# Identity products on TensorE in the two waits at the end of the last head's triangular inverse

## What is computed

```python
def gated_delta_rule(q, k, v, g, beta):
    ...
    lower = jnp.where(tri_strict, jnp.einsum('bhncd,bhnsd->bhncs', k_beta, k) * decay, 0.0)
    ...
    sol = lax.linalg.triangular_solve(lower, rhs, left_side=True, lower=True, unit_diagonal=True)
    ...

        c = depthwise_conv(c, conv_dw_w[i]) + conv_dw_b[i]
        c = jax.nn.silu(layer_norm_2(c, conv_ln_g[i], conv_ln_b[i]))
        y_conv = c @ w_conv_out[i]
        ...
        o = rms_norm_2(o_fwd + o_bwd, delta_norm_g[i]) * jax.nn.silu(z.reshape(bsz, t_len, N_HEADS, HEAD_DIM_2))
        y_delta = o.reshape(bsz, t_len, DELTA_W).astype(x.dtype) @ w_delta_out[i]
```

## Time and profile before

| | |
|---|---|
| time, median of 3 runs | 1242.95 us (1240.95 to 1244.08) |
| span of the profiled execution, first to last instruction | 1239.0 us |
| PE busy | 1211.3 us, 98% |
| DVE busy | 846.4 us, 68% |
| ACT busy | 703.4 us, 57% |
| POOL busy | 300.7 us, 24% |
| PE's share of the chain of work that ended last | 85% |

### The profile page before, as it was taken

How to read it: one execution, slowest core, us unless ns; L and a number is a source line. 1 busy time by engine, 2 the same in 40 slices (tenths; PEclk the granted TensorE clock), 3 DMA queues, 4 the chain that set the end, 5 groups by cost and what they waited for, 6 DMA issues and landing times.

```text
span 1239.0 us, 21308 instructions
## 1 busy us (share of the span) xinstructions
PE 1211.3 (98%) x8590; PEld 1109.0 (90%) x8590; DVE 846.4 (68%) x1507; ACT 703.4 (57%) x1181; POOL 300.7 (24%) x251
## 2 busy tenths in 40 slices
PE   9999999999999999999999999999999999999997
PEld 7776899998877799998899999999988989999886
DVE  6796588874675678885558787788853555555457
ACT  5465576663467566664466666767665445444344
POOL 2170100000024000000166667565645210000000
PEclk9999999999999999999989999999998999999999
DMA  7633355555553355555333232232223555555542
GB/s 282 239 140 138 119 210 194 204 186 175 180 190 108 141 210 206 196 183 203 137 136 136 103 137 103 103 137 91 83 85 116 193 187 204 194 178 197 180 159 85
DMA packets 31586, 199.74 MB, mean 161 GB/s; under 512 B 4289, under 2 KB 6481, under 8 KB 8706
## 3 DMA queue, kind: packets, MB, share of 16 engines
q1 hardware_dynamic: 29506, 189.27, 42.3%
q0 software_dynamic: 1840, 8.60, 1.8%
q10 hardware_dynamic: 144, 0.52, 0.1%
HBM read 197.33 MB, written 1.05 MB: 160 GB/s over the span
## 4 chain that ended last, share of the span: by engine, by line
PE 85%; DVE 7%; ACT 4%; issue 2%; POOL 1%; DMA 0%; POOLq 0%; SPq 0%; ACTq 0%; DVEq 0%
PE ps L1134 25%; PE ps L1136 24%; PE ps L1135 24%; PE ps L1509 1%; PE ps L1525 1%; DVE ps L2762 1%; PE ps L1287 1%; PE ps L1306 1%; PE ps L1274 1%; PE ps L1158 1%; DVE conv L2699 1%; PE ps L1141 1%; PE ps L1227 1%; DVE wlo L2314 1%; ACT whi L1784 0%
## 5 line engine op out<-in xcount | busy, mean ns | idle before, releaser
L1134 PE MATMUL ps<-halves,whi 128*128 128x256 f32 x1472 | 415.7, 282 | 0.0
L1136 PE MATMUL ps<-halves,wlo 128*128 128x256 f32 x1472 | 410.2, 279 | 0.0
L1135 PE MATMUL ps<-halves,whi 128*128 128x256 f32 x1472 | 410.1, 279 | 0.0
L2314 DVE TENSOR_TENSOR wlo<-raw,whi 128x2048 fp32r<-128x2048 f32 (+1 forms) x139 | 315.2, 2270 | 126.0 <-ACT whi L1784 122.4
L1784 ACT ACTIVATE whi<-raw 128x2048 fp32r<-128x2048 f32 (+1 forms) x143 | 270.0, 1890 | 110.9 <-PE ps L1136 106.1
L1134 PEld LDWEIGHTS ps<-halves,whi 128*128 128x128 f32 x1472 | 278.2, 189 | 0.3 <-issue 0.2
L1135 PEld LDWEIGHTS ps<-halves,whi 128*128 128x128 f32 x1472 | 278.0, 189 | 0.1
L1136 PEld LDWEIGHTS ps<-halves,wlo 128*128 128x128 f32 x1472 | 277.9, 189 | 0.0
L1075 POOL TENSOR_TENSOR wlo<-raw,whi 128x1024 fp32r<-128x1024 f32 x72 | 173.9, 2425 | 53.5 <-ACT whi L1793 53.1
L1134 PE MATMUL ps<-whi,halves 128*128 128x512 f32 (+4 forms) x440 | 151.8, 345 | 3.8 <-DVE halves L2416 3.6
L971 POOL TENSOR_TENSOR rstd<-sumsq,half_power 128x1 f32<-128x1 f32 x14 | 11.1, 796 | 594.2 <-ACT xn L1811 422.4
(11 more groups left out here) (333 smaller groups left out, 1821.5 us busy)
## 6 DMA issues: line engine op xcount, KB each, us to landing
raw<-in_stream SPq DMA_DIRECT2D x176, 1024.0 KB, 4.8
gain<-in_gains POOLq DMA_DIRECT2D x7, 512.0 KB, 6.1
bias<-in_rel POOLq DMA_DIRECT2D x1, 1536.0 KB, 9.0
raw<-in_stream SPq DMA_DIRECT2D x2, 648.0 KB, 7.3
cst<-in_consts POOLq DMA_DIRECT2D x1, 1280.5 KB, 5.9
raw<-in_stream SPq DMA_DIRECT2D x2, 528.0 KB, 4.1
x<-in_x SPq DMA_DIRECT2D x2, 512.0 KB, 4.4
out<-xn SPq DMA_DIRECT2D x4, 256.0 KB, 2.2
```

Of the source, the lines that this page charges most:

```text
L1134: nc.tensor.matmul(out, a_hi, b_hi, start=start, stop=False)
L1135: nc.tensor.matmul(out, a_hi, b_lo, start=False, stop=False)
L1136: return nc.tensor.matmul(out, a_lo, b_hi, start=False, stop=stop)
L2314: dve.tensor_tensor(used(wlo, n), used(raw, n), used(whi, n).bitcast(F32), ALU.subtract)\
```

## The change

In tick 7 of the last head's inverse, five identity products are put ahead of the wait in front of the check product, and eight ahead of the waits in front of the correction. They write PSUM bank 7.

```diff
@@ -532,6 +532,7 @@
 AB_SPINS = (6, 2)
+END_SPINS = (5, 8)
@@ -1540,6 +1541,8 @@
                     level_step(h, STEPS_FIRST[i])
                 if i == 7:
 
+                    if h == HEADS - 1:
+                        spin(END_SPINS[0], 7)
                     pe.wait_ge(*S["inverse_done"].at(h))
                     for y in range(4):
                         last = nc.tensor.matmul(ps[:, 4, y * P:(y + 1) * P], upper[:, h % 2, y, :], inv[:, y, :].bitcast(F32),
@@ -1555,6 +1558,8 @@
                 if i == 7:
+                    if h == HEADS - 1:
+                        spin(END_SPINS[1], 7)
                     pe.wait_ge(*S["residual"].at(h))
                     pe.wait_ge(*S["inverse_t"].at((h, 7)))
```

## The result

| | before | changed |
|---|---|---|
| median of 9 runs each | 1243.32 us (1240.95 to 1248.64) | 1233.99 us (1232.01 to 1238.46) |
| span of the profiled execution | 1239.0 us | 1230.7 us |

What follows compares the result with a forecast made beforehand. PE was taken to bound the kernel, with its clock at half for 6.8 us behind two waits. Products cost nothing and the held clock gives 2.2 us: 1242.95 - 2.2 = 1240.8 us, range 1238.9 to 1243.6.

Steps and rivals of the forecast that it cites:

- The two waits take the products at no cost: PE's waits ahead of L1545 and L1561: room 1.22 and 1.95 us, products 1.11 and 1.78 us, so cost nothing.
- a delay of L1545 by less than 1 us would be hidden: At the check product L1545: DVE's L2901 holds L2816 until 937.40, so a delay below about 1 us moves nothing.
- The clock is held: From 934 to 946 us: products in the waits keep the clock at 1.00, removing a fall of 6.8 us.
- there was nothing to gain in most executions: At the two waits: timed runs may keep their clock already, or products may not hold it; 1242.9 us, chance 0.17.
- 2.2 us and not 2.69, since DVE and ACT are late next: L1561 to L1591: clock alone gives at most 2.69 us; DVE's pairs and ACT's `values` limit the gain to 2.2.
- The two small waits for pairs 2 and 3 and the one for `values`: After the correction: PE waits 0.4 us and a few hundredths for DVE's L2901, and once for ACT's `values`.
- the reason given as a bound: At the edited place: a fall of 3.4 us over work instead would leave a gain of 1.2 us.
- What PE gains there it keeps: From 940 us to the end PE waits only twice, 0.5 and 0.3 us, so the gain near 940 lasts.
- How the numbers follow: Whole kernel: chances of 0.12 faster, 0.03 slower, 0.85 within about 0.3% (3.7 us); range 1238.9 to 1243.6 us.
- the start of its sum: Whole kernel: the timed median before the change, 1242.95 us, from which 2.2 was taken to get 1240.8.
- The median stands 3.9 us above the span: Whole kernel: timed median 1242.95 us against a profiled span of 1239.0; the 3.9 was added to the forecast span 1236.8.
- the whole 2.7 us, or more: At the edited place: DVE and ACT less tight, or the fall longer; 1240.2 us, 1239 with scatter, chance 0.15.

Runs made afterwards that it cites:

- the two pairs: Kernel before against the change, both with 20 identity products a layer (1262.9, 1260.5 us), then both with one (1248.7, 1247.8 us).
- the run with mixed kinds: Changed kernel plus extra products of different kinds at the start of 15 of 20 weight slots of each feed-forward layer; read from the trace alone, no time given.
- one product a layer: One identity product in slot 3 of each feed-forward layer's first matrix, added to the kernel before (mean 1248.7 us) and to the changed one (1247.8 us).

## Why the prediction was right at the place and wrong in the time

- *The two waits take the products at no cost*: right. Ten records from 932.94 and sixteen from 935.09, and the distance from L1532 to L1566 is 4.54 us, where 4.6 was forecast. Only the remark beside it, that a delay of L1545 by less than 1 us would be hidden, failed: with twice the products such a delay showed in full.
- *The clock is held*: right. It is 1.00 here in all 13 traces with products in at least one of the two waits, and it fell in all four without, each time for 6.8 us. (At 620 us one reading was a little off: 0.94 in 626 to 628 us puts the clock's return at 626.2, not 626.1. Nothing rests on it.) The rival that there was nothing to gain in most executions is answered by the time at half clock, 6.0 us less in the mean.
- *2.2 us and not 2.69, since DVE and ACT are late next*: right, 2.19. The two small waits for pairs 2 and 3 and the one for `values` are in the trace: L1135 at 939.68 and 940.46 with 0.38 instead of 0.28 us, and L1596 after ACT's L2135. In the mean over executions the gain is somewhat less, 1.6 by the two pairs (standard error 0.4). The time at half clock fits the reason given as a bound, that in some of them the fall is shorter or missing.
- *What PE gains there it keeps*: right as far as can be told. The pairs with a fixed pace have it at the end, 0.9 and 2.4 us.
- *How the numbers follow*: this step failed, by the size of its scatter term and by the start of its sum. The prediction allowed "some 0.7 us of scatter in a median of such runs", from three runs 3.1 us apart. The standard deviation of one run is 3.6 to 4.4 us. A median of nine has about 1.25 x 4.4 / 3 = 1.8 us of error, and the difference of two such medians 2.5. The start of the sum, a median of three of 1242.95, stands 2.6 us above the mean of all 136 runs. The changed kernel's nine came out on the other side, their median 3.4 below the mean of its 45. Three runs could not show that, but the trace could have: it held two paces of the same matmul, 0.113 at 930 us and 0.118 at 950, and three runs of 936 that lie on one or the other, 4.2 us each. I read the clock and the idle time, and not the distance between matmuls.
- *The median stands 3.9 us above the span*: this was a sign of the same. In the executions that have both numbers, the time stands 1.8 us above the span in the median and 2.2 in the profiled one of the changed kernel (1232.94 against 1230.7). The other 2 us say that the profiled execution was quicker than the median one.
- The rival "the whole 2.7 us, or more" lay nearer to the measured time, but not by its mechanism: DVE and ACT were as tight as their rows said.

Of the first 9.3 us, some 2 are the change. In the two traces the rest is seen: the paces behind the place, and the fall at 620 us ahead of it. In the medians it is luck: of the nine first runs of the kernel before none came below 1240.95, and of its 127 later ones 70 did, within 1233.0 to 1251.2. For nine independent draws from those 127 that has a chance of about 1 in 2000, so it was probably not plain scatter alone, but also what the executions of one group have in common. What that is, no run here shows.

## To carry to other kernels

Identity products in PE's waits pay when a pair of waits of 1 to 2 us lets the clock fall, and their size is found from rows: a wait plus 0.17 us, divided by 0.222 us for a 128-column fp32 product. Each one beyond that costs its 0.22 us in full, in the first of two waits too. Before a change of 0.2% is measured, look at how a long run of equal matmuls is paced in two traces of the same kernel. If it differs, fix it with one identity product near its start in both kernels and compare those, for the comparison alone, since it fixes the slow pace (4 us a layer here). And compare only runs that were measured together.

## What the runs showed of the hardware

- A run of weight products (fp32r, 128x128 by 256 columns) goes at 0.113 or at 0.118 us a matmul, at a granted clock of 1.00 in both cases. All 36 unbroken runs of 936 kept their pace. Of 17 runs of 240, 13 went from 0.118 to 0.113 where their operands change, without a wait.
- One identity product between them turned 0.113 into 0.118 in all eight places where the products ahead of it were at 0.113 (three layers of the run with mixed kinds, five with one product a layer). Behind four PE transposes, where the operands also change places, 0.113 became 0.118 in 27 places of 27, and behind four more it came back. Which of these does it wasn't tried.
- One and the same program gives either pace, in different layers of one execution and in the same layer of different ones.
- The clock fell to half behind two waits of 1.05 and 1.78 us that were 1.2 us of work apart, in four traces of four, for 6.8 us each time. The total time at half clock suggests that the wait of 1.78 us alone sufficed in some executions (15.5 us in the mean against 11.8 with the change) and that the wait of 1.05 us alone added nothing (11.9). In the one trace of each the clock held.
